# Decoder layer on one core: a reordered head, its first modulation chunk in halves of 256 columns, and VectorE taking 4 of 16 row tiles of the later chunks

## What is computed

```
mod = silu(c) @ w_ada + b_ada                 # 9 x 2048 values: shift, scale, gate three times
h = rms_norm(x, norm_ffn1) * (1 + sc1) + sh1
x = x + 0.5 * g1 * (silu(h @ w1_gate) * (h @ w1_up)) @ w1_down
h = rms_norm(x, norm_mix) * (1 + sc2) + sh2
x = x + g2 * token_mixing(h)                  # MLA heads and NSA heads, with a relative bias
h = rms_norm(x, norm_ffn2) * (1 + sc3) + sh3
x = x + 0.5 * g3 * (silu(h @ w2_gate) * (h @ w2_up)) @ w2_down
out = rms_norm(x, norm_final)
```

## Time and profile before

| | |
|---|---|
| median of 3 runs | 2054.48 us (2054.35 to 2056.19) |
| profiled execution, span | 2052.7 us |
| what lies around it (median less span) | 1.8 us |
| TensorE busy | 2019.7 us, 98% |
| VectorE busy | 1393.5 us, 68% |
| ScalarE busy | 876.4 us, 43% |
| DMA, mean | 260 GB/s |

### The profile page before, as it was taken

The page is one execution under the profiler, slowest core; times in us unless marked ns, Lnnn a source line. Parts: engine busy times, 40 slices in busy tenths (PEclk is TensorE's granted clock), DMA queues, the critical chain, the costliest instruction groups (busy, mean ns, idle before and its releaser), DMA issues.

```text
span 2052.7 us, 26825 instructions
## 1 busy us (share of the span) xinstructions
PE 2019.7 (98%) x9299; PEld 1602.7 (78%) x9299; DVE 1393.5 (68%) x1852; ACT 876.4 (43%) x1127; POOL 36.6 (2%) x56
## 2 busy tenths in 40 slices
PE   7999999999999999999999999999999999999998
PEld 4668888788888888787787878788888888888886
DVE  3557878877778888996556669777774455445454
ACT  4334344344443333543445644544444444434343
POOL 0000000000000000000005000000000000000000
PEclk8999999999999999999999999999999999999999
DMA  9988988899899889798966148599986677676654
GB/s 359 386 314 308 355 318 297 282 299 279 275 320 327 309 308 343 234 367 282 295 195 240 42 147 303 165 281 291 294 249 195 193 206 203 194 217 199 199 185 134
DMA packets 341269, 533.10 MB, mean 260 GB/s; under 512 B 80825, under 2 KB 95252, under 8 KB 340280
## 3 DMA queue, kind: packets, MB, share of 16 engines
q1 hardware_dynamic: 340280, 527.81, 77.8%
q10 hardware_dynamic: 896, 4.06, 0.5%
HBM read 520.04 MB, written 3.89 MB: 255 GB/s over the span
## 4 chain that ended last, share of the span: by engine, by line
PE 94%; DVE 2%; issue 1%; ACT 1%; DMA 1%; ACTq 0%; SPq 0%
PE ps L810 29%; PE ps L812 29%; PE ps L811 29%; PE ps L854 2%; PE ps L839 1%; PE ps L872 1%; DVE ada_acc L1903 1%; PE ps L1333 1%; PE ps L1336 1%; PE ps L1363 1%; DVE w_lo L1885 1%; PE ps L1168 0%; PE ps L1058 0%; ACT w_hi L1457 0%; DMA raw<-in_w_uq_dram 0%
## 5 line engine op out<-in xcount | busy, mean ns | idle before, releaser
L1457 ACT ACTIVATE w_hi<-raw 128x1024 fp32r<-128x1024 f32 (+1 forms) x657 | 689.1, 1054 | 931.5 <-PE ps L812 554.7
L1885 DVE TENSOR_TENSOR w_lo<-raw,w_hi 128x1024 fp32r<-128x1024 f32 (+1 forms) x657 | 796.4, 1220 | 402.4 <-ACT w_hi L1457 398.3
L810 PE MATMUL ps<-w_hi,hT_hi 128*128 128x512 f32 (+1 forms) x1856 | 742.0, 400 | 7.2 <-DVE hT_lo L2020 4.3
L812 PE MATMUL ps<-w_hi,hT_lo 128*128 128x512 f32 (+1 forms) x1856 | 732.1, 394 | 0.0
L811 PE MATMUL ps<-w_lo,hT_hi 128*128 128x512 f32 (+1 forms) x1856 | 732.0, 394 | 0.0
L810 PEld LDWEIGHTS ps<-w_hi,hT_hi 128*128 128x128 f32 x1856 | 350.0, 189 | 102.1 <-issue 14.2
L812 PEld LDWEIGHTS ps<-w_hi,hT_lo 128*128 128x128 f32 x1856 | 350.1, 189 | 83.8
L811 PEld LDWEIGHTS ps<-w_lo,hT_hi 128*128 128x128 f32 x1856 | 350.4, 189 | 80.0 <-issue 0.5
L1903 DVE SCALAR_TENSOR_TENSOR ada_acc<-ada_raw,silu_c,ada_acc 128x512 f32<-128x512 f32 x420 | 315.6, 751 | 8.1
L810 PE MATMUL ps<-w_hi,actT_hi 128*128 128x512 f32 x704 | 280.0, 398 | 0.0
L812 PE MATMUL ps<-w_hi,actT_lo 128*128 128x512 f32 x704 | 279.1, 396 | 0.0
(11 more groups left out here) (235 smaller groups left out, 929.7 us busy)
## 6 DMA issues: line engine op xcount, KB each, us to landing
ada_raw<-in_w_ada_dram SPq DMA_DIRECT2D x224, 512.0 KB, 5.6
raw<-in_w_gate_dram SPq DMA_DIRECT2D x176, 512.0 KB, 4.8
raw<-in_w_up_dram SPq DMA_DIRECT2D x176, 512.0 KB, 5.0
raw<-in_w_down_dram SPq DMA_DIRECT2D x176, 512.0 KB, 4.8
raw<-in_w_in_dram SPq DMA_DIRECT2D x72, 512.0 KB, 5.8
ada_half<-in_w_ada_dram SPq DMA_DIRECT2D x16, 2048.0 KB, 12.7
raw<-in_w_out_dram SPq DMA_DIRECT2D x32, 512.0 KB, 5.0
actT_lo<-norm_tmp SPq DMA_DIRECT2D x240, 32.0 KB, 3.2
```

Source lines behind the costliest of these rows:

```text
L810: pe.matmul(bank, lhs_hi, rhs_hi, start=start, stop=False)
L812: return pe.matmul(bank, lhs_lo, rhs_hi, start=False, stop=stop)
L1457: act.activation(part(U, w_hi, s), part(U, raw, s), ACT.Copy).then_inc(hi_done, 1)
L1885: dve.tensor_tensor(part(U, w_lo, s), part(U, raw, s), part(U, w_hi, s).bitcast(F32), ALU.subtract)\
```

## The change

- x is loaded first, in two DMAs by row tile, from SyncE's queue. ScalarE squares it tile by tile (`first_squares`), tile 0 before it makes silu(c).
- The small DMAs of ScalarE change their order and their semaphores; rel_bias and the bucket table come before pe_cmp_k and pe_cmp_v.
- Chunk 0 is loaded in two parts of 256 columns and 16 row tiles (2 MB each, in two DMAs with rows of 1 KB), the second part after panels 0 and 1. `start_part`, `add_part`, `turn_part` and `scale_part` do for 256 columns what was done for 512. The second part is worked inside the loop, around panel 1.
- The nine bias rows are made before chunk 0 on TensorE, and VectorE copies them.
- In each of chunks 1 to 7 VectorE takes row tiles 0 to 3 (`add_own`, four operations like L1903: acc = ada_half * silu_c + acc), two before `w_lo` of the chunk's first panel and two after it. TensorE leaves these 4 of 16 tiles out, and `add_start` adds what it made to acc. An odd half from h5 on waits for `add_own` before it is loaded.
- Some semaphores are joined into one (pads_set, side_turned, kc_copied, rows_set).

```diff
 # SyncE
+                if i > HALF_RING and i % 2 == 1:
+                    sp.wait_ge(acc_step, START_STEPS * ((i - HALF_RING) // 2) + DVE_TILES)
+                if q == 0:
+                    for b in range(2):
+                        ks = slice(b * HALF, (b + 1) * HALF)
+                        sp.dma_start(ada_half[:, i, :].rearrange("p (k n) -> p k n", k=KD)[:, ks, :],
+                                     w_ada_t[:, ks, col + i * PART:col + (i + 1) * PART]).then_inc((part_landed, half_landed)[b][i], 16)
+                    return
...
+            for t in range(TT):
+                sp.dma_start(x_sb[:, t, :], x_t[:, t, :]).then_inc(x_landed[t], 16)
             load_half(0)
-            load_half(1)
             for i in range(START_CHUNKS):
                 for j in range(4):
+                    if (i, j) == (0, 2):
+                        load_half(1)
                     gate_up(0)(Unit("gu0", i // 4), i % 4 * 4 + j)
 # TensorE
-                for kk in range(HALF):
+                own = DVE_TILES * (q > 0)
+                for kk in range(own if i % 2 == 0 else 0, HALF):
                     k, g = i % 2 * HALF + kk, kk % 4
                     mm = pe.matmul(ps[32 * g:32 * g + 32, ROW_BANK[q % 2], :], silu_pad[:, k, :],
-                                   ada_half[:, i % HALF_RING, kk * CW:(kk + 1) * CW], start=k < 4, stop=k >= KD - 4)
+                                   ada_half[:, i % HALF_RING, kk * CW:(kk + 1) * CW], start=k < own + 4, stop=k >= KD - 4)
...
-            start_half(0)
-            pe.wait_ge(rel_rep_set, 1)
+            pe.wait_ge(rows_set, 4)
             bias_rows(0, HEADS + 1)
-            start_half(1)
-            pe.wait_ge(ones_set, 1)
+            start_part(0, 0)
+            pe.wait_ge(rows_set, 3)
             spread_rstd("ffn1", T_BANK)
-            turn_start(0)
+            start_part(0, 1)
+            turn_part(0)
             pe.wait_ge(rstd_b_done, 1)
             turn_norm("ffn1", 0, x_tile)
+            start_part(1, 0)
...
-                first_panel(i, 1)
+                if i == 0:
+                    start_part(1, 1)
+                first_panel(i, 1, (lambda t: turn_part(1) if t == 1 else None) if i == 0 else None)
 # VectorE
+            def add_own(q, ks):
...
+                    dve.scalar_tensor_tensor(acc[:, a, :], ada_half[:, i % HALF_RING, k * CW:(k + 1) * CW],
+                                             silu_c[:, k:k + 1], b_row[:, a, :] if k == 0 else acc[:, a, :],
+                                             ALU.mult, ALU.add).then_inc(acc_step, 1)
...
+            copy_bias_rows()
             norm_x("ffn1")
-            add_start(0)
+            add_part(0)
+            scale_part(0)
+            first_tmp(0)
             start_lo(0, 0)
-            sum_start(0)
-            first_scale(0)
-            first_tmp(0)
             first_low(0)
             start_lo(0, 1)
+            add_part(1)
+            scale_part(1)
             first_tmp(1)
...
             for i in range(1, START_CHUNKS):
+                add_own(i, (0, 1))
                 start_lo(i, 0)
+                add_own(i, (2, 3))
                 if i >= LATE_SHIFT:
                     first_tmp(2 * i)
                 start_lo(i, 1)
```

More of the change, by code:

```diff
@@ L60 @@
 START_STEPS = 9
+DVE_TILES = 4
+PART_STEPS = 4
+PART = CW // 2
 HALF = KD // 2
@@ L163, in count_chunks @@
             if stage in ("start", "dn0", "win", "mid") or (stage == "late" and u > 0):
-                before[q] = (uses[a], last[a], None if last[a] is None else steps[last[a]] + 1)
+                taken = START_STEPS if last[a] is not None and last[a] < START_CHUNKS else 1
+                before[q] = (uses[a], last[a], None if last[a] is None else steps[last[a]] + taken)
             else:
@@ L426, in decoder_layer @@
         acc_turned, mod_done = sem("acc_turned"), sem("mod_done")
-        const_landed, x_landed, rel_landed = sem("const_landed"), sem("x_landed"), sem("rel_landed")
-        rel_set, rel_rep_set = sem("rel_set"), sem("rel_rep_set")
-        ones_set, rows_set = sem("ones_set"), sem("rows_set")
+        const_landed, rel_landed = sem("const_landed"), sem("rel_landed")
+        x_landed = [sem(f"x_landed{t}") for t in range(TT)]
+        part_turned, pe_landed = sem("part_turned"), sem("pe_landed")
+        rel_set = sem("rel_set")
+        rows_set = sem("rows_set")
         v_turned, v_done, silu_c_done = sem("v_turned"), sem("v_done"), sem("silu_c_done")
@@ L488, in decoder_layer @@
         half_used = sem("half_used")
+        part_landed = [sem(f"part_landed{i}") for i in range(2)]
         half_landed = [sem(f"half_landed{s}") for s in range(HALF_RING)]
@@ L1664, in down_unit @@
                         x_squares(("mix", "final")[f], res[U.stage]["x_added"], before(U))
[L1667 to L1673, removed]
+            act.wait_ge(rows_set, 3)
             load_root_table()
[L1675 to L1678, removed]
+            first_squares(1)
             root("ffn1", TT)
+            copy_rstd("ffn1", T_BANK)
             def start_hi(i, e):
@@ L1910, in add_start @@
                 dve.wait_ge(half_used, 2 * q + 2)
[L1911 to L1915, removed]
+                if q == 0:
+                    dve.wait_ge(b_landed[a], 16)
+                    dve.tensor_tensor(acc[:, a, :], ps[:, ROW_BANK[a], :], b_row[:, a, :], ALU.add)\
+                       .then_inc(acc_step, START_STEPS)
+                else:
+                    dve.wait_ge(acc_step, START_STEPS * q + DVE_TILES)
+                    dve.tensor_tensor(acc[:, a, :], ps[:, ROW_BANK[a], :], acc[:, a, :], ALU.add)\
+                       .then_inc(acc_step, START_STEPS - DVE_TILES)
+            def add_own(q, ks):
+                a, i = q % 2, 2 * q
+                for k in ks:
+                    if k == 0:
+                        dve.wait_ge(half_landed[i % HALF_RING], 16 * (i // HALF_RING + 1))
+                        dve.wait_ge(b_landed[a], 16 * (ADA_BEFORE[q][0] + 1))
+                        if ADA_BEFORE[q][1] is not None:
+                            dve.wait_ge(acc_turned, ADA_BEFORE[q][1] + 1)
+                    else:
+                        dve.wait_ge(acc_step, START_STEPS * q + k)
+                    dve.scalar_tensor_tensor(acc[:, a, :], ada_half[:, i % HALF_RING, k * CW:(k + 1) * CW],
+                                             silu_c[:, k:k + 1], b_row[:, a, :] if k == 0 else acc[:, a, :],
+                                             ALU.mult, ALU.add).then_inc(acc_step, 1)
             def sum_ada(U, e):
```

101 lines of the change are left out of this document (73 added, 28 removed).

## The result

The changed kernel takes 2061.03 us (median of 6 runs, 2060.58 to 2061.89); the kernel before, run beside it on the same chip, 2054.41 (6 runs, 2052.34 to 2056.19). The ratio is 1.003, with an interval of 1.002 to 1.004: slower by 6.6 us. The forecast of 2054.7 with its range up to 2057.8 was wrong, on the side to which it had given 9 in 100.

What follows compares the result with a forecast made beforehand. TensorE was taken as the bound, with DMA only 3.4 us behind in the head. Earlier start -1.4, 1 KB rows +2.0 and turn -0.35 gave +0.25 us, so 2054.7 us, range 2049.7 to 2057.8.

Steps and rivals of the forecast that it cites:

- TensorE's work: Chunks 1 to 7: 4 of 16 row tiles leave TensorE, saving 0.89 us per chunk, 6.2 us in all.
- From p28 to the turn: Chunk 7: the turn waits for VectorE and comes 6.4 us after p28 lands instead of 6.75, a gain of 0.35.
- Start of the stream: Start of the head: x needs no wait, so SyncE's load queue starts earlier, a gain of 1.4 us (0.7 to 1.6).
- Rows of 1 KB: Loads of chunk 0 in 256 columns: the shorter rows cost DMA 2.0 us (0 to 2.8).
- The rival that had them free: Chunk 0's loads: rows of 1 KB cost nothing, giving -1.75 us and 2052.7, still inside 0.2%; 15 in 100.
- The first panel: Head: p0 starts on TensorE at about 28.5 us instead of 32.52, 4 us earlier.
- In front of p0, thus in the 8 us that TensorE could be later without harm: Nine bias copies moved to VectorE cost nothing: by TensorE alone the head ends at 152.0, against 160.1.
- The queue stays fed: SyncE's load queue: p27 is issued at 120.58 and due at 123.2, so waiting for w_lo does not starve it.
- The sum: End of the head: -1.4 + 2.0 - 0.35 = +0.25 us, no change that can be measured.
- The change does not do what it says: Head: p0 not earlier, as constants or rel_bias land late; 4 us lost stay covered, 2054.7; 5 in 100.
- The slower rival, TensorE's clock: Head: the new wait in each chunk makes TensorE's clock fall, costing 1.4 us each time: +4.9, 2059.4; 9 in 100.
- DMA at 385 or more in every window: Sign that the forecast holds: DMA keeps at least 385 GB/s in every window to about 138 us.

Runs made afterwards that it cites:

- b_xfirst: Kernel before with only x loaded first by SyncE, in two DMAs, and squared half by half on ScalarE: 2057.46 us, ratio 1.0016.
- b_1kb: Kernel before with chunk 0's two half loads fetched by two DMAs each, of 256 columns (1 KB rows): 2055.77 us, ratio 1.0004.
- a_best: Changed kernel, VectorE reordered: w_lo of p2, p3 before chunk 0's second part; add_own, add_start before later chunks' first w_lo; chunks 1-3's fourth w_lo earlier: 2051.98 us, 0.9983.
- a_no_own: Changed kernel without add_own, TensorE again multiplying all 16 row tiles of chunks 1 to 7: 2060.11 us, ratio 1.0023.
- b_pad: Kernel before with nine unused VectorE additions put ahead of w_lo of p2 and p3 in chunk 0: 2061.30 us, ratio 1.0025.

## Why the prediction was wrong, step by step

**TensorE's work: right.** start_half with 12 tiles took 2.78 us in place of 3.64, 0.86 less against 0.89.

**From p28 to the turn: right.** 6.34 us, predicted 6.4, and TensorE does wait for VectorE there (3.8, the longest, in an early chunk, 0.6 in the last). So most of what was saved on TensorE was given back in that wait, as written.

**Start of the stream: right in size, worth nothing.** 126 GB/s more over 4 us is 1.3 us (1.4 predicted), but in b_xfirst nothing of it reaches p28, which hangs on p6.

**Rows of 1 KB: mis-sized.** 1.3 us in b_1kb, 2.0 taken, inside the bounds of 0 to 2.8. The rival that had them free (2052.7) falls.

**The first panel: wrong by 5.2 us.** p0 started at 33.67, not at 28.5. The bias rows took 11.88 in place of 8.5 (3.4), the last copy behind them brings norm_x to 23.44 in place of 19.5 (0.5 more), from there to the add it was 5.4 in place of 5.2, and from the add to p0 4.8 in place of 3.8, with a further part product between.

**"In front of p0, thus in the 8 us that TensorE could be later without harm": the step that failed.** The cover was reckoned along TensorE, from p0 to the end of the head. But p0 also stands ahead of the w_lo of p2, which frees the buffer of p6. On that way there was no cover at all: the kernel before already showed 376 and 366 GB/s in 36 to 44 us, a stretch that the prediction's rows leave out (they go from 16 to 44). On TensorE's own way a late p0 did no harm: in a_best it starts at 34.63, 2.1 us later than before, and the head ends at 158.25, 1.9 us earlier (160.12). What the runs showed in its place is a queue that ran dry: p6 was issued 6.41 us late, and p28 landed 6.15 late. Of the 6.41 us, 1.15 are p0's (33.67 against 32.52) and 5.26 the new distance from p0 to w_lo of p2 (8.77 against 3.51), that is the second half of chunk 0.

**"The queue stays fed": tested in the wrong place.** It was tested for p27, in the steady state, where it holds (387 GB/s after 56 us), and for h3, and not for p6, the first load that waits for VectorE while VectorE works on chunk 0. The prediction counted the nine copies and every wait that the diff adds; the part of the diff that did the damage adds no wait on SyncE. It puts work in front of an old one.

**The sum.** +0.25 was predicted at the end of the head, +5.80 was measured: +6.15 at p28, -0.41 to the turn, +0.06 behind it. The case "The change does not do what it says" came true for p0, which came 1.15 us later than before instead of 4 earlier; but the prediction priced it at nothing by the cover on TensorE, and it carries 1.15 of the 6.41 us of p6. How much of the 5.80 goes with the bias rows, which the profile before has short and that of the change long, stays open; by the single executions it may be about 2.

**The slower rival, TensorE's clock: not it.** It fell once, to 0.79 in 48 to 52 us and 0.78 in 52 to 56, when TensorE had run out of panels after the hole (1.38 us busy of 4): a consequence. From 56 us on no fall is seen in the windows, in spite of the waits before the turns. And a_no_own and b_pad, slow in the same way, show 1.00 from 8 to 168 us.

The prediction had named its own tests: wrong if p28 lands 3 us later, or if the clock is under 1.00 after 45 us. Both came. The first of its signs, "DMA at 385 or more in every window", points at the hole itself, and the kernel before did not pass it either (376 and 366).

## What to carry to other kernels

In a stream that is busy without a gap, every load whose buffer must first be freed has a due time; find for each stage, the first above all, which operation of which engine frees it, and what a change puts in front of that operation, even if it adds no wait. An engine's slack is not one number: here a late p0 was harmless on the way over TensorE (a_best) and cost its full length on the way over VectorE to SyncE. Put the operation that frees a buffer, or the one that the next turn waits for, first in the engine's order: moving lines alone brought 1.0030 to 0.9983 here (after and a_best).

## What was unexpected of the hardware

Bias products of 33x384 took 844 ns each in one profile and from 482 in another, while the granted clock was shown as 1.00 in both; the column does not tell every stretch at the lower level. The Trainium skill, "TensorE: Matmul & The Clock Gate", Part 1, warns that the clock events of a trace can be unreliable on this chip, and with these rows the trace agrees. The products of start_half in the kernel before say the same:

```profile
11.64 3.64 PE L854 MATMUL ps<-ada_half,silu_pad 128*32 128x512 f32 x16 [0.69 <-ACT silu_pad L1610]
23.67 3.64 PE L854 MATMUL ps<-ada_half,silu_pad 128*32 128x512 f32 x16
39.82 3.64 PE L854 MATMUL ps<-ada_half,silu_pad 128*32 128x512 f32 x32
```

From 39.82 on two halves take together what one took before, with the clock shown as 1.00. So both early ones ran at the lower level, though it is shown only for the second (0.50, and 1.00 for the first). In the first 35 us here the length of a known product tells the level where the column does not.
